# Branch products of a two-block transformer kernel in three split passes, with GpSimd making low weight parts in the mixing loop

## The reference, cut to what matters

```python
for l in range(2):                                  # 256 tokens, width 1024, f32 throughout
    x = x + 0.5 * swiglu(rms_norm(x, ...), ...)
    h = rms_norm(x, norm_g[l, 1])
    qa, ka, va, qd, kd, vd, qc, kc, vc = split(h @ w_in[l])
    ya = neighbourhood_attention(qa, ka, va, na_rpb[l])          # 8 heads
    yb = diff_attention(qd, kd, vd, lam, ..., rel_bias[:, :4])   # 4 heads of 2 maps, rms_norm per head
    yc = window_gqa(qc, kc, vc, gqa_sink[l], rel_bias[:, 4:])    # 8 heads
    g = sigmoid(h @ w_gate[l] + b_gate[l]).reshape(B, S, 3, 1024)
    merged = g[:,:,0]*(ya @ w_branch[l,0]) + g[:,:,1]*(yb @ w_branch[l,1]) + g[:,:,2]*(yc @ w_branch[l,2])
    x = x + merged @ w_o[l]
    x = x + 0.5 * swiglu(rms_norm(x, ...), ...)
# then a second block: modulated norms, attention and retention, a mixture of experts, a last norm
```

## Time and profile before

| quantity | value |
|---|---|
| median of 3 runs | 1988.19 us (1986.71 to 1988.6) |
| profiled execution, its own time | 1988.11 us |
| its span, first to last instruction | 1986.3 us |
| TensorE, matmul busy | 1938.6 us (98%) |
| VectorE busy | 1223.6 us (62%) |
| ScalarE busy | 703.3 us (35%) |
| GpSimd busy | 0.2 us |
| TensorE clock granted, mean | 0.995 of full speed |
| mixing loop of the first layer | about 306 to 447 us of the span |
| mixing loop of the second layer | about 953 to 1093 us of the span |

### The profile page before, as it was taken

How to read it: one execution, slowest core, us unless ns; L and a number is a source line. 1 busy time by engine, 2 the same in 40 slices (tenths; PEclk the granted TensorE clock), 3 DMA queues, 4 the chain that set the end, 5 groups by cost and what they waited for, 6 DMA issues and landing times.

```text
span 1986.3 us, 33632 instructions
## 1 busy us (share of the span) xinstructions
PE 1938.6 (98%) x14053; PEld 1597.6 (80%) x14053; DVE 1223.6 (62%) x2117; ACT 703.3 (35%) x1052; POOL 0.2 (0%) x4
## 2 busy tenths in 40 slices
PE   9999999999999999999999999999899999999997
PEld 9999998889999999999888999999666444433432
DVE  6665759876567877775987777767766332322221
ACT  5433436535333534453654534443332000000001
POOL 0000000000000000000000000000000000000000
PEclk9999999999999999999999999999999999999999
DMA  8798563276776677656325676654308999999996
GB/s 245 239 354 259 173 188 117 96 203 207 227 218 206 214 231 225 202 181 191 118 96 166 207 237 190 209 122 128 127 22 361 404 421 421 421 422 421 421 421 288
DMA packets 275426, 476.66 MB, mean 240 GB/s; under 512 B 29270, under 2 KB 235152, under 8 KB 250696
## 3 DMA queue, kind: packets, MB, share of 16 engines
q1 hardware_dynamic: 275020, 474.38, 69.1%
q10 hardware_dynamic: 252, 0.08, 0.0%
HBM read 473.27 MB, written 7.95 MB: 242 GB/s over the span
## 4 chain that ended last, share of the span: by engine, by line
PE 84%; DMA 8%; DVE 5%; ACT 1%; SPq 1%; issue 1%; DVEq 0%; ACTq 0%
PE ps L792 83%; DMA ring_over<-in_moe_w_up_dram 3%; DMA ring_zone<-in_moe_w_up_dram 3%; DMA hl_place<-in_moe_w_up_dram 1%; DMA ring_over<-in_moe_w_gate_dram 1%; SPq L712 1%; PE ps L1132 1%; PE ps L1275 0%; DVE PT L2365 0%; DVE WL L1990 0%; PE ps L1452 0%; DVE hl L1930 0%; ACT mT L1770 0%; ACT gT L1718 0%; DVE gT L2394 0%
## 5 line engine op out<-in xcount | busy, mean ns | idle before, releaser
L792 PE MATMUL ps<-hh,WH 128*128 128x256 f32 x2232 | 633.2, 284 | 1.3 <-DVE WL L1919 0.7
L792 PE MATMUL ps<-hl,WH 128*128 128x256 f32 x2232 | 623.0, 279 | 0.0
L792 PE MATMUL ps<-hh,WL 128*128 128x256 f32 x2232 | 622.8, 279 | 0.0
L1919 DVE TENSOR_TENSOR WL<-W,WH 128x1024 fp32r<-128x1024 f32 x390 | 471.7, 1223 | 243.6 <-ACT WH L1534 241.9
L1534 ACT ACTIVATE WH<-W 128x1024 fp32r<-128x1024 f32 x390 | 408.3, 1056 | 433.7 <-PE ps L792 406.2
L792 PEld LDWEIGHTS ps<-hh,WH 128*128 128x128 f32 x2232 | 418.9, 188 | 14.8 <-issue 11.6
L792 PEld LDWEIGHTS ps<-hl,WH 128*128 128x128 f32 x2232 | 418.7, 188 | 1.2 <-issue 1.0
L792 PEld LDWEIGHTS ps<-hh,WL 128*128 128x128 f32 x2232 | 418.8, 188 | 0.0
L792 PE MATMUL ps<-hid_h,WH 128*128 128x256 f32 x704 | 200.4, 285 | 0.0
L792 PE MATMUL ps<-hid_l,WH 128*128 128x256 f32 x704 | 197.5, 280 | 0.0
L792 PE MATMUL ps<-hid_h,WL 128*128 128x256 f32 x704 | 197.2, 280 | 0.0
(11 more groups left out here) (404 smaller groups left out, 2585.3 us busy)
## 6 DMA issues: line engine op xcount, KB each, us to landing
W<-in_ffn_w_gate_dram SPq DMA_DIRECT2D x88, 512.0 KB, 5.1
W<-in_ffn_w_up_dram SPq DMA_DIRECT2D x88, 512.0 KB, 4.7
W<-in_ffn_w_down_dram SPq DMA_DIRECT2D x88, 512.0 KB, 4.1
W<-in_w_in_dram SPq DMA_DIRECT2D x78, 512.0 KB, 4.5
ring_over<-in_moe_w_gate_dram SPq DMA_DIRECT2D x29, 1024.0 KB, 25.3
ring_over<-in_moe_w_up_dram SPq DMA_DIRECT2D x28, 1024.0 KB, 25.3
W<-in_w_gate_dram SPq DMA_DIRECT2D x48, 512.0 KB, 3.6
ring_zone<-in_moe_w_down_dram SPq DMA_DIRECT2D x24, 1024.0 KB, 26.1
```

The costliest lines, as they stand in the source:

```text
L792: ins = nc.tensor.matmul(o, lhsT, rhs, start=start, stop=stop, skip_group_check=True, **kw)
L1919: v.tensor_tensor(low, W[:, i % RAW, :], high.bitcast(F32), ALU.subtract).then_inc(low_ready, 1)
```

## The change

`w_branch` joins the split weights. Each of the 48 branch tiles becomes 12 passes in fp32r in place of 4 f32 matmuls, with `WH` and `WL` of the piece against `y_high` and `y_low` of the head outputs, which DVE makes (behind each value product for branches one and three; in eight added instructions at step 20 for branch two). GpSimd makes `WL` of all 36 pieces of `w_gate` and `w_branch` of a layer, DVE that of all others. On DVE, forms change: the negation goes into the row maximum, the sigmoid's last step into the product with the gate (the factor 0.5 moves to `mix_h` and `mix_l`), and `tensor_scalar` and `tensor_tensor` between SBUF tiles become `scalar_tensor_tensor`. `MIX_HALVES` and `MIX_RESTS` go; `used` stands at the head of a step on ACT and before the branch tile on DVE and counts branch pieces too. `load_ada` waits for 16 branch tiles.

```diff
-SPLIT = ("ffn_gate", "ffn_up", "ffn_down", "w_in", "w_gate", "w_in2", "w_o")
+SPLIT = ("ffn_gate", "ffn_up", "ffn_down", "w_in", "w_gate", "w_branch", "w_in2", "w_o")
...
+                        sp.wait_ge(merge_ready, 24 * l + 16)          # load_ada, first block of (l, 1)
...
-                        done_pair()                                    # TensorE, behind the gates
+                        if merged_tile(s) is not None and merged_tile(s) % 2 == 1:
+                            held["gates"] += 1
+                        else:
+                            done_pair()
...
-                            mm(ps[:, MERGE_BANK + j % 2, 0:T],
-                               chunk["b"][:, k * 256 + (i % 2) * P:k * 256 + (i % 2 + 1) * P],
-                               yT[:, branch * 4 + k, :], k == 0, k == 3, then=merge_ready if k == 3 else None)
+                            mm3(ps[:, MERGE_BANK + j % 2, 0:T], at(chunk["b"], k * 256 + (i % 2) * P),
+                                (y_high[branch * 4 + k], y_low[branch * 4 + k]), k == 0, k == 3,
+                                then=merge_ready if k == 3 else None)
                         if i % 2 == 1:
-                            done_plain()
+                            done_pair(1 + held["gates"])
+                            held["gates"] = 0
...
                 for s in range(MIX_STEPS):                             # ACT
+                    j = merged_tile(s)
+                    used((s < 24) + (j is not None and j % 2 == 0))
                     if s < 24:
                         b = s % 4
-                        used(1)
                         act.wait_ge(smax, due(smax))
...
-                    if s in MIX_HALVES:
-                        used(1, ahead=0)
...
-                        used(1)                                        # DVE
                     j = merged_tile(s)
+                    used((s < 24) + (j is not None and j % 2 == 0))
                     if j is not None:
                         branch, i = j // 8, j % 8
+                        dve.wait_ge(gate_ready, 12 * l + j // 2 + 1)
                         dve.wait_ge(merge_ready, due(merge_ready))
...
-                            v.tensor_tensor(rs[:, :], bank[:, 0:T], g, ALU.mult).then_inc(merge_free, 1)
+                            v.scalar_tensor_tensor(out=rs[:, :], in0=g, scalar=1.0, in1=bank[:, 0:T],
+                                                   op0=ALU.add, op1=ALU.mult).then_inc(merge_free, 1)
...
+                            link(v.tensor_copy(y_high[u // 2], ps[:, PV_BANK, 0:T]))
+                            v.tensor_tensor(y_low[u // 2], ps[:, PV_BANK, 0:T], y_high[u // 2].bitcast(F32), ALU.subtract)\
+                                .then_inc(pv_free, 1)
...
+                        for h in range(4):                             # DVE at step 20, behind L2305's four
+                            ins = v.scalar_tensor_tensor(out=y_high[4 + h], in0=yT[:, 4 + h, :], scalar=1.0,
+                                                         in1=yT[:, 4 + h, :], op0=ALU.mult, op1=ALU.min)
+                        link(ins)
+                        for h in range(4):
+                            v.scalar_tensor_tensor(out=y_low[4 + h], in0=yT[:, 4 + h, :], scalar=1.0,
+                                                   in1=y_high[4 + h].bitcast(F32), op0=ALU.mult, op1=ALU.subtract)\
+                                .then_inc(yn_ready, 1)
...
-                                ins = v.tensor_scalar(part, part, rc[:, b, q:q + 1], None, ALU.mult)
+                                ins = v.scalar_tensor_tensor(out=part, in0=part, scalar=rc[:, b, q:q + 1], in1=part,
+                                                             op0=ALU.mult, op1=ALU.min)
...
+            for l in range(DEPTH):                                     # GpSimd
+                pool.wait_ge(low_ready, pool_first[l])
+                for n in range(pool_first[l], pool_last[l] + 1):
+                    pool.wait_ge(high_ready, n + 1)
+                    high, low, _ = split_place(n)
+                    nc.gpsimd.tensor_tensor(low, W[:, split_at[n] % RAW, :], high.bitcast(F32), ALU.subtract)\
+                        .then_inc(low_ready, 1)
```

More of the change, by code:

```diff
@@ L306, in build @@
         eps_sq = sb("eps_sq", [P, 1])
+        zeros = sb("zeros", [P, TT])
         nm = sb("nm", [P, 4, 2])
@@ L394, in build @@
         cT = gT[:, 8:16, :]
+        _, QK_r, yT_r = zone(("before_QK", [P, TT * 1152], F32), ("QK_r", [P, 22, T], FR), ("yT_r", [P, 12, T], FR))
+        y_high = (*(yT_r[:, k, :] for k in range(4)), *(QK_r[:, 12 + k, :] for k in range(4)), *(yT_r[:, 8 + k, :] for k in range(4)))
+        y_low = (*(QK_r[:, 4 + k, :] for k in range(4)), *(yT_r[:, 4 + k, :] for k in range(4)), *(QK_r[:, 16 + k, :] for k in range(4)))
         nT = flat(T5[:, :, :])[:, 0:2048].rearrange("p (k t) -> p k t", k=KD)
@@ L558, in build, with split_by_pool @@
         plain_no = {i: n for n, i in enumerate(i for i in range(len(plan)) if i not in split_no)}
+        pool_first = [split_no[plan.index(("w_gate", l, 0, 0))] for l in range(DEPTH)]
+        pool_last = [split_no[plan.index(("w_branch", l, 11, 0))] for l in range(DEPTH)]
+        def split_by_pool(n):
+            return any(pool_first[l] <= n <= pool_last[l] for l in range(DEPTH))
         in2_at = split_no[plan.index(("w_in2", 0, CHUNK[ORDER[0]], 0))]
@@ L1082, in head_values @@
                                k == 0, k == 1, then=pv_ready if k and e else None)
+                held = {"gates": 0}
                 for s in range(MIX_STEPS):
@@ L1729, in _ @@
                         act.wait_ge(dn_sums, due(dn_sums))
-                        nc.scalar.activation(QK[:, 5, :], ps[:, PV_BANK, 0:T], ACT.Sqrt, bias=eps[:, :],
+                        nc.scalar.activation(QK[:, 8, :], ps[:, PV_BANK, 0:T], ACT.Sqrt, bias=eps[:, :],
                                              scale=1.0 / P).then_inc(dn_root, 1)
-                    if s in MIX_HALVES:
-                        used(1, ahead=0)
-                    j = merged_tile(s)
                     if j is not None and j >= 16:
                         act.wait_ge(m_ready, due(m_ready))
-                        nc.scalar.activation(mix_h[:, j - 16, :], mT[:, j - 16, :], ACT.Copy).then_inc(mix_high, 1)
-                used(2, ahead=0)
+                        nc.scalar.activation(mix_h[:, j - 16, :], mT[:, j - 16, :], ACT.Copy, scale=0.5).then_inc(mix_high, 1)
+                used(4, ahead=0)
                 round_and_square(lambda k: col("norm_g", l * 24 + 16 + k), mixed=True)
@@ L1916, in rests @@
                     i = split_at[n]
+                    if split_by_pool(n):
+                        st["split"] += 1
+                        continue
+                    if n and split_by_pool(n - 1):
+                        dve.wait_ge(low_ready, n)
                     dve.wait_ge(high_ready, n + 1)
@@ L1966, in mixed_low @@
                 dve.wait_ge(mix_high, due(mix_high))
-                v.tensor_tensor(mix_l[:, k, :], mT[:, k, :], mix_h[:, k, :].bitcast(F32), ALU.subtract)\
-                    .then_inc(mix_low, 1)
+                v.scalar_tensor_tensor(out=mix_l[:, k, :], in0=mT[:, k, :], scalar=0.5, in1=mix_h[:, k, :].bitcast(F32),
+                                       op0=ALU.mult, op1=ALU.subtract).then_inc(mix_low, 1)
             def norm_factor():
@@ L2317, in _ @@
                         if branch == 2:
-                            link(v.tensor_tensor(sm[:, b, :], sm[:, b, :], es[:, b, :], ALU.add))
+                            link(v.scalar_tensor_tensor(out=sm[:, b, :], in0=sm[:, b, :], scalar=1.0, in1=es[:, b, :],
+                                                        op0=ALU.mult, op1=ALU.add))
                         link(v.reciprocal(rc[:, b, :], sm[:, b, :]))
                         if branch == 1 and i % 2 == 1:
-                            link(v.tensor_scalar(rc[:, b, :], rc[:, b, :], neglam[:, l:l + 1], None, ALU.mult))
+                            link(v.scalar_tensor_tensor(out=rc[:, b, :], in0=rc[:, b, :], scalar=neglam[:, l:l + 1],
+                                                        in1=zeros[:, :], op0=ALU.mult, op1=ALU.add))
                         for q in range(TT):
@@ L2332, in _ @@
                             dve.wait_ge(p_ready, l * 24 + s + 1)
-                        if s % 2 == 1:
-                            dve.wait_ge(gate_ready, due(gate_ready))
-                            g = flat(gT[:, (branch % 2) * 8 + i - 1:(branch % 2) * 8 + i + 1, :])
-                            link(v.tensor_scalar(g, g, 0.5, 0.5, ALU.mult, ALU.add))
-                    if s in MIX_RESTS:
-                        used(1, ahead=0)
+                due(gate_ready, 12)
                 mixed_low(KD - 1)
-                used(2, ahead=0)
+                used(4, ahead=0)
                 update_mixed(1.0, lambda k: col("norm_g", l * 24 + 16 + k))
@@ L2784, in _ @@
         def _(pool):
-            pass
```

(2 more changed lines are left out.)

36 lines of the change are left out of this document (21 added, 15 removed).

## The result

| | before | after |
|---|---|---|
| median, us | 1988.39 (1986.71 to 1990.48, 4 runs) | 2058.44 (2056.65 to 2060.24, 4 runs) |
| profiled span, us | 1986.3 | 2054.5 |
| clock granted, mean | 0.995 | 0.985 |

The ratio is 1.035 [1.0338, 1.0362]: 70 us slower, where I had said 10.7 slower (1999) and 2022 at most.

What follows compares the result with a forecast made beforehand. TensorE was taken to bound the mixing loop. Per layer, net of its saving, 1.1 us up to tile 15 plus 4.25 in the tail made 5.35, 10.7 in two, giving 1999 us; range 1984 to 2022, likeliest case 1992 to 2005.

Steps and rivals of the forecast that it cites:

- the order: Both layers' loop and tail: waits from the new instruction order, less TensorE's saving, cost 5.35 us a layer, 10.7 in two.
- What bounds, and the saving: Mixing loop: TensorE bounds; branch tiles shrink from 1.72 to 1.41 us, saving 7.4 a layer, 15 in all at most.
- GpSimd's 2.4 us, at no cost: GpSimd's 36 low parts a layer take 2.4 us each, below the 2.8 us under which nothing waits.
- Blocking: Rival: DVE operations reading two SBUF tensors and GpSimd's subtractions block each other; 22 us more, 2021; chance 0.18.
- The two-source forms: DVE's 40 divisions a layer, in the new form, grow from 351 to about 482 ns, 5.2 us, no cost.
- Step 18: First new wait: two splits ahead of map 18 make ACT's square end, and head sums start, 1.45 us later.
- Steps 19 and 20: Lateness carried through step 19's split, table load and map puts DVE's step-20 scalings at 405.3 instead of 403.69.
- the burst: Step 20: twelve DVE operations instead of four stand before tile 8, which starts 3.8 us late.
- the bare 2.2: Step 20: tile 8's delay, 2.2 us, even if DVE began its scalings as early as before.
- Steps 21 to 24: Loop's end: waits take back tiles 8 to 11's saving; tile 12 about +4.2, tile 15's end 1.1 us later.
- the ring: Loop, no forecast term: split waits for TensorE, exponentials for the split, division for them, TensorE for the division.
- The tail: Behind tile 15: late `w_o` transfer and low parts stop TensorE before tiles 20 and 22; costs 4.25 us a layer.

Runs made afterwards that it cites:

- g1: The changed kernel with its new 8-byte tensor `zeros` laid into unused space of `mx`, so later tensors keep the earlier kernel's addresses; 2035.39 us, ratio 1.0231.
- h1: e1 with the SBUF addresses of the kernel before the change; 2024.51 us, ratio 1.0182.
- f3: f2 with GpSimd again making the low parts of `w_gate` and `w_branch`; 2056.85 us, ratio 1.0334.
- f2: f1 with the first `w_ada` block waiting for 8 branch tiles instead of 16; 2025.96 us, ratio 1.018.
- e1: The changed kernel with DVE making all low parts and GpSimd doing nothing; 2046.16 us, ratio 1.029.
- f1: e1 with ACT and DVE splitting up to 2 pieces ahead in the mixing loop instead of 3; 2025.71 us, ratio 1.0188.
- h4: f2 at old addresses, step-20 rounding on ACT, tail low parts behind tile reads, one-input divisions, ACT rounding `y_high` of branches one and three; 1987.04 us.
- e3: e1 plus two unneeded GpSimd fills, only writing SBUF, at each of a layer's 36 pieces; 2046.36 us, ratio 1.0296.

## Why the prediction was wrong, point by point

The 70 us come apart as a chain of runs: after to g1 23.0 (addresses), g1 to h1 10.9 (blocking, less what DVE's added load costs), h1 to before 36 (order, with the low parts on DVE). The forecast had only the order, at 10.7.

- **What bounds, and the saving.** Right. After, a branch tile's twelve passes take 432.95 to 434.39, 1.44 us; in h1, at the old addresses, 1.42 (354.69 to 356.11). I said 1.41. Up to the end of step 18's gates h1 needs 81.55 us from the loop's first transposes where before needed 83.44, the 1.9 that I took off for tiles 0 to 5.
- **GpSimd's 2.4 us, at no cost.** The size was right (2415 ns), the "no cost" wrong by at least 10.9. Blocking was a rival at 0.18 and 22 us. I gave it too little: my own argument against it was none, only that no row spoke of it. Its net price lies on both sides of my 22: 11 here, 31 in an order with fewer other waits (f3 less f2).
- **The two-source forms.** The division in e1 is 482 ns, as the earlier trace rows said. By the Trainium skill (Vector Engine (DVE) Microarchitecture Reference, Points that are easy to get wrong) it would be up to twice as long; the trace disagrees.
- **Step 18.** Right in kind, 0.8 short: in h1 the head sums start 4.68 us behind the end of the step's gates (388.26 to 392.94), I said 3.9.
- **Steps 19 and 20.** The first failure: "DVE's four scalings at 405.3", with the gates of step 18 ending at 389.01. In h1 they start at 409.72, or 410.5 on that clock, 5.2 later. I had the terms (split behind tile 7, table load, exponentials) but not that TensorE's gates of step 19 themselves take 3.94 us at the low clock instead of 2.93, and so the tile that the split waits for is late. Of the 5.2, 0.8 are step 18's, 1.0 the gates', and 2.4 are two low parts of DVE ahead of the scalings (401.23 and 408.58), which the forecast had on GpSimd. Tile 8's own wait for the burst was 2.59, near the bare 2.2.
- **Steps 21 to 24: the step that failed.** "Tile 12 at about +4.2", and the end of tile 15 at +1.1. In h1 tile 12 starts at 436.95 against 424.97, which is +12.7 on the forecast's clock (step 18's gates together). Tile 15 ends at about 445.6 against 433.0, +11.5 counted from the start of the loop, where I had 1.1. Each lateness was taken back in my sum by the next step's saving. In the run it was not. At step 19 the ring closes: ACT's split waits 4.98 us for TensorE's tile 7, the exponentials stand behind it, and DVE idles 5.69 us (its row above). f1 opens the ring by one slot and gives 20 us back. From there on h1's DVE has no time to catch up: the stop of 5.11 us at step 24 ends with ACT's copy at 435.50, which stands behind a tanh that waited 3.11 us for DVE's gate scaling. How much of the 12.7 the ring gives alone, and how much the 8.5 us of low parts that DVE has here and not in the forecast, stays open. That DVE's load counts in these steps, h4 shows.
- **The tail.** The sum was right, in part by luck: `w_ada` is issued right behind tile 15 (h1: 445.79), TensorE stands 3.85 us before tile 20 (I said 3.8), and `w_o` starts 18.5 us behind tile 15 (I said 18.0). But the first split starts at 453.39, 7.8 behind tile 15 and not 6.7, and the second stop of 2.0 us, before tile 22, doesn't come. In its place the passes behind the first stop run at the low clock, some 22 of them at 0.21 us, 2.3 us more in all.

```profile
456.18 0.55 PE L802 MATMUL ps<-yT_r,WH 128*128 128x256 f32 x1 [3.85 <-DVE rs L2308]
```

- **The clock** stood in no term: up to 8.4 us in the first layer and 13.4 in the second.
- **Addresses** stood in none either. The diff had the line, `zeros = sb("zeros", [P, TT])`, and it moved every activation tensor by 8 bytes.

The direction and its chance (0.75 slower) held, and h1 shows that it held without blocking and addresses too; the range left out every case in which two causes meet.

## What to carry to other kernels

When a change makes a full engine wait, price the ring and not the gap: follow what the waiting engine's own delay makes late, until the chain comes back to it, and add what the clock takes behind each stop; a lead one slot longer or shorter can be worth more than the work saved. GpSimd as a helper beside DVE was free here when it only wrote SBUF (e3) and never when it read; its price is DVE's stretched SBUF-to-SBUF work, less the work that it takes off DVE. And whenever a kernel gets a new tensor, look at a stretch that the change doesn't touch: if passes come at another pace there, put the tensor elsewhere before judging the rest.
